# Hybrid encoder layer with routed experts: second norm by matrix products, early routing constants, late slot weights, early down weights, bounds read between low parts

## The reference

```
proj = x @ w_in                       # queries, keys, values of three groups of heads
oa = window_attention(...)            # 8 heads, |t-s| <= 128, sink logit, ALiBi
ob = neighborhood_attention(...)      # 4 heads on an 8 x 64 grid, window 8 x 16, bias table
om = memory_attention(...)            # 4 heads over 256 memory tokens
mixed = concat(group_rms(oa), group_rms(ob), group_rms(om))
x = layer_norm(alpha * x + mixed @ w_out, ln1_g, ln1_b)
scores = sigmoid(x @ w_router)        # 16 experts in 4 groups; best group, top 2 of it
y = sum over the 2 chosen e of weight[e] * ((silu(x @ w_gate[e]) * (x @ w_up[e])) @ w_down[e])
x = layer_norm(alpha * x + y, ln2_g, ln2_b)
```

## Time and profile before

| | |
|---|---|
| three timed runs | 1030.45, 1035.67 and 1038.74 us, median 1035.67 |
| profiled execution | 1033.42 us, its span 1031.7 us |
| TensorE busy | 897.9 us (87% of the span) |
| VectorE busy | 617.6 us (60%) |
| ScalarE busy | 524.7 us (51%) |
| GpSimd busy | 186.0 us (18%) |
| moved by DMA | 187.73 MB, mean 182 GB/s |

### The profile page before, as it was taken

How to read it: one execution, slowest core, us unless ns; L and a number is a source line. 1 busy time by engine, 2 the same in 40 slices (tenths; PEclk the granted TensorE clock), 3 DMA queues, 4 the chain that set the end, 5 groups by cost and what they waited for, 6 DMA issues and landing times.

```text
span 1031.7 us, 15892 instructions
## 1 busy us (share of the span) xinstructions
PE 897.9 (87%) x4927; PEld 736.1 (71%) x4928; DVE 617.6 (60%) x1179; ACT 524.7 (51%) x976; POOL 186.0 (18%) x264
## 2 busy tenths in 40 slices
PE   5889999899889999989926899999999999999900
PEld 5766888677867788877715777777888878888800
DVE  4344633655634654556599889896545766456248
ACT  3343565542425555553353688785644856346212
POOL 4300002010000012000021244343232222223104
PEclk9999999899989999989967999999999999999965
DMA  7731114126322342301756999999877796772254
GB/s 265 141 62 41 42 51 134 42 86 197 106 62 83 123 165 82 101 23 62 266 204 224 366 375 380 363 379 370 289 219 249 252 351 209 221 242 51 56 183 163
DMA packets 111165, 187.73 MB, mean 182 GB/s; under 512 B 22801, under 2 KB 51712, under 8 KB 111120
## 3 DMA queue, kind: packets, MB, share of 16 engines
q1 hardware_dynamic: 97296, 139.48, 38.9%
q0 software_dynamic: 13824, 47.68, 17.3%
HBM read 159.33 MB, written 28.17 MB: 182 GB/s over the span
## 4 chain that ended last, share of the span: by engine, by line
PE 43%; DVE 15%; issue 8%; ACT 2%; DMA 2%; DVEq 1%; ACTq 0%; POOL 0%; POOLq 0%
PE O L1760 8%; PE C L1490 8%; PE C L1492 7%; PE C L1491 7%; DVE split_main L1412 6%; PE O L1671 3%; PE S L1525 2%; PE T L1646 2%; PE S L1726 1%; PE T L1719 1%; DVE mixing L1475 1%; PE T L1554 1%; DVE x_nat L1429 1%; DVE x_nat L1402 1%; DMA acc_dram<-x_nat,idxs 1%
## 5 line engine op out<-in xcount | busy, mean ns | idle before, releaser
L1412 DVE TENSOR_TENSOR split_main<-mixing,split_main 128x1024 fp32r<-128x1024 f32 x192 | 222.2, 1220 | 43.7 <-ACT split_main L993 40.7
L993 ACT CAST split_main<-mixing 128x1024 fp32r<-128x1024 f32 x192 | 190.5, 1049 | 19.7 <-PE C L1492 10.1
L1490 PE MATMUL C<-split_main,split_aux 128*128 128x512 f32 x368 | 143.9, 391 | 2.6 <-DVE split_aux L1418 2.6
L1491 PE MATMUL C<-split_main,split_aux 128*128 128x512 f32 x368 | 143.9, 391 | 0.0
L1492 PE MATMUL C<-split_main,split_aux 128*128 128x512 f32 x368 | 143.8, 391 | 0.0
L1490 PE MATMUL C<-split_main 128*128 128x512 f32 (+1 forms) x320 | 130.6, 408 | 9.7 <-DVE split_main L1276 6.3
L1760 PE MATMUL O<-split_main,split_aux 128*128 128x512 f32 x552 | 132.8, 396 | 0.0
L1491 PE MATMUL C<-split_main 128*128 128x512 f32 (+1 forms) x320 | 121.9, 381 | 0.0
L1492 PE MATMUL C<-split_main 128*128 128x512 f32 (+1 forms) x320 | 121.5, 380 | 0.0
L1760 PEld LDWEIGHTS O<-split_main,split_aux 128*128 128x128 f32 x552 | 100.1, 188 | 23.5 <-DVE split_aux L1433 3.4
L1490 PEld LDWEIGHTS C<-split_main 128*128 128x128 f32 x320 | 63.3, 198 | 29.0 <-issue 11.2
(11 more groups left out here) (284 smaller groups left out, 1388.5 us busy)
## 6 DMA issues: line engine op xcount, KB each, us to landing
mixing<-in_w_gate SPq DMA_DIRECT2D x64, 512.0 KB, 8.4
mixing<-in_w_up SPq DMA_DIRECT2D x64, 512.0 KB, 6.4
mixing<-in_w_down SPq DMA_DIRECT2D x64, 512.0 KB, 8.9
mixing<-in_w_in SPq DMA_DIRECT2D x20, 512.0 KB, 3.8
mixing<-in_w_out SPq DMA_DIRECT2D x16, 512.0 KB, 3.8
mixing<-in_w_mem_kv SPq DMA_DIRECT2D x8, 512.0 KB, 5.3
mixing<-in_w_in SPq DMA_DIRECT2D x16, 256.0 KB, 3.5
x_dram<-x_nat POOLq DMA_DIRECT2D x8, 512.0 KB, 3.0
```

What stands on the lines that cost most here:

```text
L993: nc.scalar.copy(wu[0][:, w, :], raw[:, w, :]).then_inc(unit_hi, 1)
L1412: nc.vector.tensor_tensor(wu[1][:, w, :], raw[:, w, :], wu[0][:, w, :].bitcast(F32), ALU.subtract).then_inc(unit_lo, 1)
L1490: ins = nc.tensor.matmul(out_ap, st[0], mvg[0], start=first, stop=False)
L1491: ins = nc.tensor.matmul(out_ap, st[0], mvg[1], start=False, stop=False)
```

## The change

- **Second norm.** Only for sequence 1: VectorE makes the first pass alone (`ln_centred`). ScalarE makes for each tile a diagonal matrix of the roots (`lnd`, event VAR), and TensorE (`norm_rows`) multiplies it with the centred rows in full precision, 512 columns at a time, and adds the bias by two products with a row of ones (high and low part of the bias). ScalarE copies the two banks back to `x_nat` (`norm_out`) and adds to `x1_ready`. Tiles 0 and 1 stand on TensorE ahead of the rank products and on ScalarE behind the sigmoid; tiles 2 and 3 stand on TensorE behind the rank products, ahead of the one-hot ones, and on ScalarE behind four high parts of expert 0. The bias row is split once in sequence 0.
- **Routing constants** are written to other places, before the first Y of the last half.
- **Slot weights**: the eight operations move from `routing` into `slot_weight_parts`, behind `routed`.
- **Down weights of expert 0**: SP loads them behind chunk 37, and the first six parts of gate and up behind chunk 38, ahead of chunk 39. Events D make their high and low parts in two pairs between the chunks. Their counts are given to `unit_hi` and `unit_lo` at once after the eighth part. VectorE makes one low part of expert 0 ahead of `xgT_los(0)`, seven behind it, and then `slot_weight_sum`; before it made three, `slot_weight_sum`, `xgT_los(0)` and nine.
- **Bounds**: on VectorE the two `value_load`s of experts 1 to 15 stand behind low parts 5 and 6, and 7 and 8.

```diff
         prepare(s, 5)
+        if s == NSEQ - 1:
+            ev.append(("D", s, (KD, KD + 1)))
...
                 inputs(s + 1, "m", (pi - 1,))
+            if s == NSEQ - 1 and pi == 0:
+                ev.append(("D", s, (KD + 2, KD + 3)))
...
     ev.append(("SC", s))
-    for t in range(UNITS // 2):
+    for t in range(KD // 2):
...
         woh = probsT[:, :, :].rearrange("p a b -> p (a b)").bitcast(BF16).rearrange("p (a b) -> p a b", a=2 * TT)
+        consts = probsT[:, :, :].rearrange("p a b -> p (a b)")
+        rev4, thr = cut(consts, 0, TT * NG, EG), cut(consts, P, NE, TT)
+        one16, tnum = consts[:, 2 * P:2 * P + NE], consts[:, 2 * P + NE:2 * P + NE + TT]
+        bias_hi, bias_lo, one_row = RX[0:1, 0:D], RX[0:1, D:2 * D], RX[0:1, 2 * D:2 * D + P]
+        lnd = [probs[:, 1, t * P:(t + 1) * P] for t in range(3)] + [probs[:, 0, P:2 * P]]
...
             return ([Cb[0], Cb[1], Ob[0], Sb[0]], [Sb[1], Ob[1], Ob[0], Sb[0]])[half][t]
+        def ln_bank(t, half):
+            return ([Cb[0], Cb[1]], [Sb[0], Sb[1]])[t % 2][half]
...
             nc.vector.memset(seed[:, 9:10], 0.0).then_inc(norm_ready, 1)
+        def routing_constants(link):
+            for i in range(EG):
+                nc.vector.memset(rev4[:, :, i], float(EG - i))
+            for i in range(TT):
+                nc.vector.memset(thr[:, :, i], float(P * i))
+            nc.vector.memset(one16, 1.0)
+            link(nc.vector.tensor_scalar(tnum, tokf[:, :], tokf[:, 0:1], 1.0 / P, ALU.subtract, ALU.mult))
+            link(nc.vector.tensor_scalar(tnum, tnum, float(TT), None, ALU.subtract))
...
             lo_p = rows8[:, 640:640 + SLOTS]
-            rev4 = w16[7]
-            thr = cut(rows8, 384, NE, TT)
-            one16, tnum = rows8[:, 560:576], rows8[:, 624:632]
-            for i in range(EG):
-                nc.vector.memset(rev4[:, :, i], float(EG - i))
-            for i in range(TT):
-                nc.vector.memset(thr[:, :, i], float(P * i))
-            nc.vector.memset(one16, 1.0)
-            link(nc.vector.tensor_scalar(tnum, tokf[:, :], tokf[:, 0:1], 1.0 / P, ALU.subtract, ALU.mult))
-            link(nc.vector.tensor_scalar(tnum, tnum, float(TT), None, ALU.subtract))
...
             tmp = cut(rows16, 384, TT, NE)
-            w_a, w_b, w_s = w8[2], w8[3], w8[4]
-            link(nc.vector.tensor_tensor(tmp, E1, sc[:, :, :], ALU.mult))
-            link(nc.vector.tensor_reduce(w_a, tmp, AX.X, ALU.add))
-            link(nc.vector.tensor_tensor(tmp, E2, sc[:, :, :], ALU.mult))
-            link(nc.vector.tensor_reduce(w_b, tmp, AX.X, ALU.add))
-            link(nc.vector.tensor_tensor(w_s, w_a, w_b, ALU.add))
-            link(nc.vector.reciprocal(w_s, w_s))
-            link(nc.vector.tensor_tensor(wts[:, 0, :], w_a, w_s, ALU.mult))
-            link(nc.vector.tensor_tensor(wts[:, 1, :], w_b, w_s, ALU.mult))
...
         def slot_weight_parts(link):
+            E1, E2 = cut(rows16, 128, TT, NE), cut(rows16, 256, TT, NE)
+            tmp = cut(rows16, 384, TT, NE)
+            w8 = [rows8[:, 256 + 8 * i:256 + 8 * (i + 1)] for i in range(8)]
+            w_a, w_b, w_s = w8[2], w8[3], w8[4]
+            link(nc.vector.tensor_tensor(tmp, E1, sc[:, :, :], ALU.mult))
+            link(nc.vector.tensor_reduce(w_a, tmp, AX.X, ALU.add))
+            link(nc.vector.tensor_tensor(tmp, E2, sc[:, :, :], ALU.mult))
+            link(nc.vector.tensor_reduce(w_b, tmp, AX.X, ALU.add))
+            link(nc.vector.tensor_tensor(w_s, w_a, w_b, ALU.add))
+            link(nc.vector.reciprocal(w_s, w_s))
+            link(nc.vector.tensor_tensor(wts[:, 0, :], w_a, w_s, ALU.mult))
+            link(nc.vector.tensor_tensor(wts[:, 1, :], w_b, w_s, ALU.mult))
...
                     sp.dma_start(slot, part).then_inc(chunk_loaded[g % 2], 16)
-            for g in range(NSEQ * NCH):
-                load_chunk(g)
-                if g == 1:
-                    for t in range(NT):
-                        sp.dma_start(x_nat[:, t, :], x[0][t * P:(t + 1) * P, :]).then_inc(x_loaded[0][t], 16)
...
                     sp.dma_start(raw[:, w, :], src.rearrange("a p c -> (a p) c")).then_inc(raw_loaded[w], 16)
-            sp.wait_ge(biased, 2 * (32 + 16))
-            for w in range(UNITS):
-                if w == 6:
-                    sp.wait_ge(chunk_lo, NSEQ * NCH)
+            for g in range(NSEQ * NCH):
+                load_chunk(g)
+                if g == NSEQ * NCH - 3:
+                    u = T_OF_MIXED[("oB", NSEQ - 1, NT - 1)]
+                    sp.wait_ge(t_ready[u % 2], u // 2 + 1)
+                    for w in range(KD, UNITS):
+                        load_unit(0, w)
+                if g == NSEQ * NCH - 2:
+                    sp.wait_ge(biased, 2 * (32 + 16))
+                    for w in range(6):
+                        load_unit(0, w)
+                if g == 1:
+                    for t in range(NT):
+                        sp.dma_start(x_nat[:, t, :], x[0][t * P:(t + 1) * P, :]).then_inc(x_loaded[0][t], 16)
+            sp.wait_ge(chunk_lo, NSEQ * NCH)
+            for w in (6, 7):
...
+
+            def norm_out(t):
+                act.wait_ge(ln_psum, t + 1)
+                for half in range(2):
+                    ins = nc.scalar.copy(x_nat[:, t, half * 512:(half + 1) * 512], ln_bank(t, half)[:, :])
+                ins.then_inc(x1_ready, 1)
...
                                          ACT.Copy).then_inc(t_drained[u % 2], 1)
+                elif what == "LN" and s == 0 and ev[2] == 0:
+                    act.wait_ge(ln_loaded, 32)
+                    nc.scalar.copy(bias_hi, ln[0:1, 1, :]).then_inc(bias_rows, 1)
+                    nc.scalar.copy(one_row, ones_b[0:1, :]).then_inc(bias_rows, 1)
+                elif what == "VAR" and s == NSEQ - 1:
+                    act.wait_ge(root_ready, 1)
+                    for t in range(NT):
+                        nc.scalar.activation(lnd[t], ident[:, :], ACT.Copy, scale=rstd[:, s * NT + t:s * NT + t + 1])\
+                            .then_inc(diag_ready, 1)
...
+                    for t in range(2):
+                        norm_out(t)
+                elif what == "D":
+                    for w in ev[2]:
+                        act.wait_ge(raw_loaded[w], 16)
+                        nc.scalar.copy(wu[0][:, w, :], raw[:, w, :]).then_inc(down_hi, 1)
...
+                    if t == 2:
+                        for n in (2, 3):
+                            norm_out(n)
...
+                    if t == KD // 2 - 1:
+                        act.wait_ge(down_hi, KF)
+                        nc.scalar.copy(warm[:, :], fzero[:, :]).then_inc(unit_hi, KF)
...
                     pos, g = WO_ORDER[half].index(t), s * NCH + WO0 + half * 4 + 3
+                    if s == NSEQ - 1 and half == 1 and pos == 0:
+                        routing_constants(link)
...
                                             .to_broadcast([P, NT, 2, HD]), ALU.mult).then_inc(o_drained[gi % 2], 1)
+                elif what == "D":
+                    for w in ev[2]:
+                        dve.wait_ge(down_hi, w - KD + 1)
+                        nc.vector.tensor_tensor(wu[1][:, w, :], raw[:, w, :], wu[0][:, w, :].bitcast(F32), ALU.subtract)\
+                            .then_inc(down_lo, 1)
...
+                    if s == NSEQ - 1:
+                        nc.vector.memset(seed[:, 11:12], 0.0).then_inc(root_ready, 1)
...
                         dve.wait_ge(ln_loaded, 32)
+                        dve.wait_ge(bias_rows, 2)
+                        nc.vector.tensor_tensor(bias_lo, ln[0:1, 1, :], bias_hi.bitcast(F32), ALU.subtract).then_inc(bias_rows, 1)
...
+                    if s == NSEQ - 1:
+                        nc.vector.scalar_tensor_tensor(row, row, mvv[:, t, 0:1], ln[:, 0, :], ALU.subtract, ALU.mult)\
+                            .then_inc(ln_centred, 1)
+                        continue
...
             def expert(e, first=False, last=False):
+                if not first:
+                    lo_units(e, range(5, 7))
...
+                if not first:
+                    lo_units(e, range(7, 9))
...
-                    lo_units(e, range(5, UNITS))
+                    lo_units(e, range(9, UNITS))
...
             slot_weight_parts(link)
-            lo_units(0, range(3))
+            lo_units(0, range(1))
+            xgT_los(0)
+            lo_units(0, range(1, KD))
+            dve.wait_ge(down_lo, KF)
+            nc.vector.memset(seed[:, 10:11], 0.0).then_inc(unit_lo, KF)
...
-            xgT_los(0)
-            lo_units(0, range(3, UNITS))
...
                     nc.tensor.matmul(Tb[u % 2][:, 0:NE], lgT[:, :], sel16[:, :], start=True, stop=True).then_inc(t_ready[u % 2], 1)
+            def norm_rows(t):
+                pe.wait_ge(ln_centred, t + 1)
+                pe.wait_ge(diag_ready, t + 1)
+                if t == 0:
+                    pe.wait_ge(bias_rows, 3)
+                if t >= 2:
+                    pe.wait_ge(x1_ready, NT + t - 1)
```

(11 more changed lines are left out.)

7 lines of the change are left out of this document (added).

## The result

| | before | after |
|---|---|---|
| timed runs, median (range) | 1035.68 us (1030.45 to 1038.74, 4 runs) | 1047.45 us (1045.49 to 1050.96, 4 runs) |
| profiled execution, its span | 1033.42, 1031.7 us | 1045.49, 1043.8 us |

The ratio is 1.0136, with an interval of 1.0100 to 1.0172: slower by 1.4%. It comes from the stretch that the change works on, and most of it from one step for which I had the right place and the wrong size.

The account below looks back on a forecast made before the run. It took VectorE to bound the early experts, with the weight stream catching up by 700 us. 1033.42 + 1.3 - 0.65 = 1034.1 us, given as 1035.3 from the mean of four times; range 1030.0 to 1040.5.

Parts of the forecast that it names:

- Norm on TensorE: Second norm ahead of the routing: four second passes leave VectorE, but routing waits for GpSimd's iota; 0.8 us gained, not 4.3.
- The new wait on the stores: GpSimd's first gather waits for the last normed-row stores, landing at 546 to 547.1; transposes near 552, 0.7 us late.
- rival 2: norm_rows at half clock, TensorE 534 to 544: list or stores 2 to 4 us late, 4 us slower, 1038.5; chance 0.2.
- Constants early, weights late: Routing: moved constants give nothing; moved slot weights gain 0.6 us at the list, then cost 2.1 us ahead of woh_ready.
- Down weights early: Expert 0's loads around chunk 39: covered by 1 us; 16.0 against 15.8 us to first product; weight stream 1.5 us late.
- rival 4: Early loads delay chunk 39 past 502: 1 to 2 us slower; chance 0.05.
- Bounds between low parts: One-tile experts: idle 0.63 us goes, 18.73 becomes 18.10 us; weight stream still makes product 7 1.3 us late; expert 11 gives 0.65.
- Rival 1: Early experts: weight stream keeps up, product 7 at 699.0, 4 us faster in all, 1031.3; chance 0.22.
- The sum: Whole kernel: 1033.42 + 1.3 - 0.65 = 1034.1 us, 1035.3 as forecast; nothing else in the end stage changes.

Follow-up runs that it names:

- no_norm: The changed kernel with both passes of the second norm on VectorE again, all else kept: 1036.18 us, ratio 1.0013 to the kernel before.
- full_bias: The changed kernel with the norm's one-row bias products made 128-row fast-format products of other data, full-precision product kept: 1042.84 us, ratio 1.0116 to the kernel before.
- weights_back: no_norm with the eight slot-weight operations in `routing` again: 1031.63 us, a single run.
- bounds_only: The kernel before with only the two bound reads moved between low parts: 1031.16 us, ratio 0.9979.
- half_down: bounds_only with half of the rows of each down part loaded for experts 1 to 15: 1053.02 us, a single run.
- best: order_back with expert 1's down weights loaded as soon as expert 0's are split: 1031.51 us, ratio 0.9952 to the kernel before.
- order_back: weights_back with three low parts of expert 0 and the slot weights' sum ahead of the split of the rows again: 1031.72 us, ratio 0.9976.

## Why the prediction was wrong, by its steps

I forecast 1035.3 us and a range to 1040.5; it is 1047.45. In the table times count from the span's start, and the first norm pass starts 0.12 us later in after than in before.

| step | forecast | measured |
|---|---|---|
| routing starts, just behind the iota | 526.0 | 529.63 |
| a tile of `norm_rows` | 2.6 us | 6.3 us |
| rank products end | 533.8 | 537.3 |
| norm_rows(3) ends | 540.3 | 549.8 |
| list | 545.0 | 551.84 |
| last store lands | 546 to 547.1 | 556.4 |
| transposes start | 552 | 562.25 |
| product 0 | 572.3 | 582.50 |
| product 7 | 703.6 | 714.35 |

**The step that failed is the size of a `norm_rows` tile**, in two places of "Norm on TensorE" and "The new wait on the stores". I priced it at full clock, 2.6 us, allowed 0 to 1.7 us for the clock at the first pair and 1.2 us (between 0 and 5.3) at the second. TensorE had half its clock for all four tiles, which no_norm (the loss gone without these products) and full_bias (6.2 us back at the first multiplication, with the clock at full level for part of the stretch) show to be the cause. Twice 2.6 is 5.2 of the 6.3. The rest lies in both kinds of product: the full-precision one takes 1.98 us up to the start of the one-row product behind it (521.76 to 523.74) against twice 0.86, and a one-row product, for which I had bounds of 0.23 and 0.39 us at full clock, 0.57 (523.74 to 524.33 to 524.88) against twice 0.23, where a 128-row product of fast format takes 0.43.

**The chain was right and its ends were not.** The routing does start just behind the iota, and not at 522.6; the gather does follow the stores. But with tiles of 6.3 us another queue decides that I had named only in rival 2: the 16 one-hot products stand behind norm_rows(3) on TensorE. Their operands were ready at 546.27, they ran at 549.78. That rival had the mechanism, half level in `norm_rows`, at a chance of 0.2. It allowed for it in the second pair alone, gave 544.3 for the end of norm_rows(3) and 551 for the stores, and so 4 us. Counted from the first norm pass, the routing starts 2.6 us late, the list adds 2.8, the gather 4.6 and the way to the first multiplication 0.9 us. The trace of before would have told more than I took from it: the granted clock is at 0.61 in 522 to 524, and no row there shows one-row products bringing it back; I took full clock for all of them because it was the level ahead of the fall.

**Constants early, weights late** went as forecast: 0.6 us gained at the list and 1.2 us net lost at the first multiplication (forecast 2.1 - 0.6 = 1.5), by no_norm against weights_back. In after the transposes wait for the gather in any case.

**Down weights early.** Chunk 39 landed at 501.77, where I had 501, and its first sum stood at 506.41, where before had 506.38: covered, and rival 4 is out. From the first multiplication to product 0 it is 15.74 us against 15.67, so nothing was gained there, as forecast (16.0 against 15.8). That the order of the low parts was to blame, and 2.9 us were to be had, I did not see; nor that fewer loads behind the gather shorten it.

**Bounds between low parts.** The first three experts take 18.13 us, and expert 11 as well, 18.13 for 18.75: 0.62 us, where I had 0.65. In after the later periods take it back: product 7 comes 131.85 us behind product 0, where I had 131.3 and before had 130.94. bounds_only, with nothing else late, has gained 1.3 us at product 7 (129.64) and has lost it again at product 8. Rival 1, that the stream keeps up, did not come: 371 GB/s at a share of 1.05 in 620 to 700, as before, not the 435 GB/s that the Trainium skill (DMA: Bandwidth & Descriptors, "Where 436 GB/s comes from") names as the fabric's ceiling. (The same section gives some 358 GB/s for one core's share of the HBM; these rows lie above it.) That the stream is the cause rests on these rows and on periods that grow where ScalarE waits on a load. It is argued: half_down was to show it by itself and did not, and best gained less at product 7 than the bytes taken out of the stream would give.

**The sum.** 12.1 us lie between the profiled executions, against 0.7 in my sum. Of the difference of 11.4 us, 10.2 are there at product 0 (582.50 against 572.3) and 0.55 more at product 7. Behind it come 0.3 us, since most periods are 18.13 us and not 18.10, and 0.4 us in the end stage, in which nothing was changed. The chance for slower by over 1%, 0.04, was too low for a change that puts 24 products (four tiles of two halves with three products each) and the waits of two other engines ahead of the routing and the gather: each piece had an unfavourable bound, and no case held them together.

## What to carry to other kernels

Before moving a step to TensorE in a stretch where it is nearly idle, read the granted clock there, and price the step at half level for its whole length unless a row shows such products bringing the clock back. A step that frees one engine's time is worth nothing if its result now comes through three engines to a wait ahead of the same consumer: walk every semaphore that the old step gave, and every product queued behind the new ones. When a period is longer than its neighbours, follow the wait back to the first operation that is late and compare its duration with that in other periods: in order_back TensorE waited for a gather that was as quick as ever, behind one index operation that took 7.6 us in place of 1. And look whether an experiment has removed what it was to remove: half_down halved the bytes of some loads and left the DMA engines as full as before.
